# A hybrid trunk layer's expert weights, loaded as four neighbouring rows per partition instead of four rows 128 apart

## What is computed

```python
def expert_choice_ffn(x, w_router, w1, w3, w2):
    cap = EC_FACTOR * T // N_EXPERTS
    aff = jax.nn.softmax(jnp.einsum('btd,de->bte', x, w_router).astype(F32), axis=-1)
    gval, idx = lax.top_k(jnp.swapaxes(aff, 1, 2), cap)
    xs = jax.vmap(lambda xb, ib: xb[ib])(x, idx)
    hid = jax.nn.silu(jnp.einsum('becd,edf->becf', xs, w1)) * jnp.einsum('becd,edf->becf', xs, w3)
    yo = jnp.einsum('becf,efd->becd', hid, w2) * gval[..., None].astype(x.dtype)
    ...
def trunk_layer(x, mod, lp, li, ctx):
    shift1, scale1, gate1, shift2, scale2, gate2 = [mod[:, i, None, :] for i in range(6)]
    h = rmsnorm(x, lp['g_norm1']) * (1 + scale1) + shift1
    mix, new_ctx = token_mixers(h, lp, li, ctx)
    x = x + gate1 * mix
    h2 = rmsnorm(x, lp['g_norm2']) * (1 + scale2) + shift2
    x = x + gate2 * expert_choice_ffn(h2, lp['w_router'], lp['w_e1'], lp['w_e3'], lp['w_e2'])
```

## Time and profile before

| | us |
|---|---|
| median of three runs | 2092.44 |
| lowest and highest run | 2089.23, 2095.91 |
| span of the profiled execution | 2094.6 |
| TensorE busy in it | 1974.3 (94%) |
| expert part of layer 0, first expert product to the end of the last | 572.2 to 1044.4 |
| expert part of layer 1 | 1610.2 to 2081.5 |

### The profile page before, as it was taken

How to read it: one execution, slowest core, us unless ns; L and a number is a source line. 1 busy time by engine, 2 the same in 40 slices (tenths; PEclk the granted TensorE clock), 3 DMA queues, 4 the chain that set the end, 5 groups by cost and what they waited for, 6 DMA issues and landing times. The chain is left out here.

```text
span 2094.6 us, 19778 instructions
## 1 busy us (share of the span) xinstructions
PE 1974.3 (94%) x7810; PEld 896.4 (43%) x7810; DVE 478.2 (23%) x1254; ACT 355.3 (17%) x920; POOL 21.8 (1%) x40
## 2 busy tenths in 40 slices
PE   6999999989899999999979999999898999999997
PEld 2464444454533433433335544544545343334332
DVE  1043224353300100100020612254523011001002
ACT  2123222411200100100021231223112010001000
POOL 0000000000000000000000000000000000000000
PEclk8999999989799999999989999999897999999999
DMA  9141113343799999999952412035346999999996
GB/s 370 61 166 66 60 41 121 152 172 120 264 364 409 396 410 410 409 410 410 409 202 67 165 60 80 21 121 201 123 162 259 377 410 397 410 410 409 410 410 264
DMA packets 136068, 532.95 MB, mean 254 GB/s; under 512 B 5121, under 2 KB 5249, under 8 KB 136001
## 3 DMA queue, kind: packets, MB, share of 16 engines
q1 hardware_dynamic: 134448, 527.59, 64.2%
q0 software_dynamic: 1552, 4.44, 0.6%
HBM read 529.13 MB, written 2.88 MB: 254 GB/s over the span
## 5 line engine op out<-in xcount | busy, mean ns | idle before, releaser
L562 PE MATMUL bank<-ring,hT 128*128 128x512 f32 (+2 forms) x1440 | 598.8, 569 | 3.4 <-DMA ring<-in_w_in 2.1
L562 PE MATMUL bank<-ring,scr 128*64 128x512 f32 (+1 forms) x2176 | 525.9, 597 | 33.8 <-DMA ring<-in_w_e 16.5
L562 PE MATMUL bank<-scr 128*64 128x512 f32 (+6 forms) x2048 | 522.2, 520 | 7.9 <-DVE dsm L1726 4.7
L562 PEld LDWEIGHTS bank<-ring,hT 128*128 128x128 f32 x1440 | 268.7, 191 | 272.2 <-issue 266.1
L562 PEld LDWEIGHTS bank<-scr 128*64 128x64 f32 (+3 forms) x2048 | 213.1, 164 | 295.4 <-issue 287.0
L562 PEld LDWEIGHTS bank<-ring,scr 128*64 128x64 f32 (+1 forms) x2176 | 177.1, 142 | 353.5 <-issue 316.7
L1869 DVE TENSOR_TENSOR scr<-scr,bank 128x512 f32<-128x512 f32 x32 | 22.0, 687 | 627.8 <-ACT scr L1384 627.8
L571 PE MATMUL bank<-cst,scr 128*128 128x128 f32 (+1 forms) x530 | 92.2, 290 | 21.2 <-DVE scr L1764 8.4
L571 PEld LDWEIGHTS bank<-cst,scr 128*128 128x128 f32 (+1 forms) x530 | 58.5, 142 | 101.1 <-issue 70.7
L1384 ACT ACTIVATE scr<-bank 128x512 f32<-128x512 f32 x32 | 19.1, 597 | 467.8 <-PE bank L562 467.8
L562 PE MATMUL bank<-ring,csw 128*32 128x512 f32 x384 | 59.9, 768 | 30.4 <-DMA ring<-in_w_ada 17.7
(11 more groups left out here) (206 smaller groups left out, 1016.6 us busy)
## 6 DMA issues: line engine op xcount, KB each, us to landing
ring<-in_w_e SPq DMA_DIRECT2D x124, 2048.0 KB, 18.2
scr<-in_w_e SPq DMA_DIRECT2D x64, 2048.0 KB, 16.7
ring<-in_w_ada SPq DMA_DIRECT2D x24, 2048.0 KB, 9.7
ring<-in_w_in SPq DMA_DIRECT2D x20, 2048.0 KB, 8.1
ring<-in_w_br SPq DMA_DIRECT2D x8, 1024.0 KB, 7.1
ring<-in_w_out SPq DMA_DIRECT2D x4, 2048.0 KB, 8.8
ring<-in_w_in SPq DMA_DIRECT2D x4, 1552.0 KB, 16.4
ring<-in_w_in SPq DMA_DIRECT2D x4, 1536.0 KB, 6.9
```

What stands on the lines that cost most here:

```text
L562: ins = pe.matmul(out, lhsT, rhs, start=start, stop=stop, **kw)
```

## The change

A half of an expert's matrix is now read with `w.rearrange("(p k) n -> p (k n)", k=4)`: partition p gets rows 4p to 4p + 3, which are 16 KB in one run. The product of chunk k then sums over rows 4p + k, so everything that is multiplied with such a chunk is taken at every fourth element: the helper `quads(ap, k)` gives channels 512h + 4p + b (k = 4h + b). It is applied to the stationary pieces of `xn` in `gather`, to the pieces of `xn` that `widths("h2T")` transposes, and to the row results in `columns(3)` and `columns(4)`; `hid` is written as before and its transposes take every fourth column. The router's weights and the columns of the experts' norm (g_norm2 and two biases) must be in the same order: `wr` is loaded in runs of four rows, and a new tile `cq` gets its 24 columns by 24 small transfers per layer on GpSimd's queue, of 32 partitions x 4 elements, each element 288 B from the next in HBM. VectorE waits for them (`params_second`) ahead of `columns(3)`. No computation is added or left out.

```diff
@@ -155,6 +155,7 @@
         cp = sb("cp", [P, NCOL])
+        cq = sb("cq", [P, 3, KD])
         ca = sb("ca", [P, NCACHE])
@@ -249,7 +250,7 @@
         hs = exp_take(HALF)
-        hid = exp_take(HALF).rearrange("p (b n) -> p b n", b=4)
+        hid = exp_take(HALF).rearrange("p (n b) -> p n b", b=4)
         hidT = exp_take(HALF).rearrange("p (b n) -> p b n", b=4)
@@ -274,6 +275,10 @@
         banks = [ctx.enter_context(nc.psum_tensor(f"bank{i}", [P, 512], F32)) for i in range(8)]
+
+        def quads(ap, k):
+
+            return ap[:, (k // 4) * HALF:(k // 4 + 1) * HALF].rearrange("p (n b) -> p b n", b=4)[:, k % 4, :]
@@ -311,6 +316,7 @@
         params = sem("params")
+        params_q = sem("params_second")
         kv_out = sem("kv_out")
@@ -438,7 +444,11 @@
                         base = li * PER[s]
-                    load(base + before, s, (w_e1, w_e3, w_e2)[s // 2][li, e, (s % 2) * HALF:(s % 2 + 1) * HALF, :], D)
+                    w = (w_e1, w_e3, w_e2)[s // 2][li, e, (s % 2) * HALF:(s % 2 + 1) * HALF, :]
+                    if not (isinstance(base + before, int) and base + before == 0):
+                        sp.wait_ge(freed[s], base + before)
+                    sp.dma_start((ring[:, s] if s < SLOTS else more[:, s - SLOTS]).rearrange("p k n -> p (k n)"),
+                                 w.rearrange("(p k) n -> p (k n)", k=4)).then_inc(loaded[s], 16)
@@ -450,8 +460,8 @@
                     for k in range(4):
-                        r = s * HALF + k * P
-                        sp.dma_start(chunk(SLOTS_E + s, k), w_e1[li, 1, r:r + P, :]).then_inc(loaded[SLOTS_E + s], 16)
+                        rows4 = w_e1[li, 1, s * HALF:(s + 1) * HALF, :].rearrange("(p k) n -> k p n", k=4)
+                        sp.dma_start(chunk(SLOTS_E + s, k), rows4[k]).then_inc(loaded[SLOTS_E + s], 16)
                 for e, slots in ((2, (0, 1)), (1, (2, 3, 4, 5)), (2, (2, 3, 4, 5))):
@@ -500,7 +510,13 @@
                 pool.dma_start(ca[:, :], caches[li, :, :]).then_inc(params, 16)
-                pool.dma_start(wr[:, :, :], w_router[li, :, :].rearrange("(k p) e -> p k e", p=P)).then_inc(params, 16)
+                pool.dma_start(wr.rearrange("p (h b) e -> p h b e", h=2), w_router[li, :, :].rearrange("(h p b) e -> p h b e", h=2, b=4)).then_inc(params, 16)
+                for a in range(4):
+                    for i, c0 in enumerate((COLS["gn2"][0], COLS["bada"][0] + 16, COLS["bada"][0] + 24)):
+                        for h in range(2):
+                            src = colp[li, :, c0 + 4 * h + a].rearrange("(q b) -> q b", b=4)
+                            pool.dma_start(cq[32 * a:32 * a + 32, i, 4 * h:4 * h + 4], src,
+                                           allow_slow_non_contiguous=True).then_inc(params_q, 16)
@@ -619,7 +635,7 @@
                     for k in range(KD):
-                        mm(b[:, 2 * k:2 * k + 2], rsb[:, v % 2, k * P:(k + 1) * P], c_("sel"),
+                        mm(b[:, 2 * k:2 * k + 2], quads(rsb[:, v % 2, :], k) if v > 2 else rsb[:, v % 2, k * P:(k + 1) * P], c_("sel"),
                            signal=big if k == KD - 1 else None)
@@ -647,7 +663,7 @@
                         for t in range(NT):
-                            turn(b[:, t * P:(t + 1) * P], xn[:, t, k * P:(k + 1) * P],
+                            turn(b[:, t * P:(t + 1) * P], quads(xn[:, t, :], k) if name == "h2T" else xn[:, t, k * P:(k + 1) * P],
                                  signal=big if t == NT - 1 else None)
@@ -989,7 +1005,6 @@
                     for k in range(KD):
-                        cols = slice(k * P, (k + 1) * P)
                         b = banks[6 + k % 2]
@@ -999,11 +1014,11 @@
                             pe.wait_ge(sc_ready, 1)
-                        mm(b[:, 0:16 * n], xn[:, 0, cols], Sc[:, e0:e1, :])
+                        mm(b[:, 0:16 * n], quads(xn[:, 0, :], k), Sc[:, e0:e1, :])
                         if k == 0:
                             pe.wait_ge(hot_ready, 1)
-                        mm(b[:, 16 * n:48 * n], xn[:, 1, cols], Sl[:, 0, e0:e1, :], stop=False)
-                        mm(b[:, 16 * n:48 * n], xn[:, 2, cols], Sl[:, 1, e0:e1, :], start=False, signal=gath)
+                        mm(b[:, 16 * n:48 * n], quads(xn[:, 1, :], k), Sl[:, 0, e0:e1, :], stop=False)
+                        mm(b[:, 16 * n:48 * n], quads(xn[:, 2, :], k), Sl[:, 1, e0:e1, :], start=False, signal=gath)
@@ -1052,7 +1067,7 @@
                     for b in range(4):
-                        turn(banks[6][:, b * P:(b + 1) * P], hid[:, b, :], signal=ht_ready if b == 3 else None)
+                        turn(banks[6][:, b * P:(b + 1) * P], hid[:, :, b], signal=ht_ready if b == 3 else None)
                     if not (isinstance(e, int) and e == 0):
@@ -1491,15 +1506,17 @@
                     n = (0, 1, None, 2, 3)[v]
+                    if v == 3:
+                        dve.wait_ge(params_q, (li + 1) * 16 * 24)
                     b = grab(("col", v))
-                    bias = cp[:, COLS["bada"][0] + 8 * n:COLS["bada"][0] + 8 * n + 8]
+                    bias = cp[:, COLS["bada"][0] + 8 * n:COLS["bada"][0] + 8 * n + 8] if v < 2 else cq[:, n - 1, :]
                     gave(("col", v), V.tensor_tensor(modc[:, n, :, :], b[:, 0:16].rearrange("p (k g) -> p k g", g=2),
...
                         V.scalar_tensor_tensor(gs[:, i, :, :], modc[:, 2 * i + 1, :, :], 1.0,
-                                               rep(cp[:, 8 * i:8 * i + 8], 2, 2), ALU.add, ALU.mult).then_inc(mod1, 1)
+                                               rep(cp[:, 0:8] if i == 0 else cq[:, 0, :], 2, 2), ALU.add, ALU.mult).then_inc(mod1, 1)
                         dve.wait_ge(mod1, i + 1)
@@ -1866,7 +1883,7 @@
                     dve.wait_ge(silu_ready, e + 1)
-                    V.tensor_tensor(hid.rearrange("p b n -> p (b n)"), hs, banks[7][:, :], ALU.mult).then_inc(hid_ready, 1)
+                    V.tensor_tensor(hid.rearrange("p n b -> p (n b)"), hs, banks[7][:, :], ALU.mult).then_inc(hid_ready, 1)
                     dve.wait_ge(sg_ready, e + 2)
```

## The result

The changed kernel is slower: 2109.72 us, median of 4 runs (2105.9 to 2112.55), against 2094.18 us for the kernel before (4 runs). The ratio is 1.0071, with a 95% interval of 1.0051 to 1.009, so the change costs 0.7% where 0.7% of gain was forecast. It lies at the upper edge of the stated range, which was rival 1's 2109 us. The profiled execution took 2111.45 us, 2.1 us over its span.

What follows compares the result with a forecast made beforehand. Full DMA engines bound most of the expert part, TensorE waiting for weights; 2094.6 - 19.5 (waits) + 4.7 (transposes) = 2079.8 us profiled, 2077.6 us against the median of runs, range 2071 to 2111.

Steps and rivals of the forecast that it cites:

- rival 1: TensorE's reads at every fourth element are slow in every load, not only in transposes: 2109 us with doubled loads; chance 0.20.
- TensorE's waits as the cap of the gain: Expert parts of both layers: faster transfers can give back only TensorE's waits for weights, 19.5 us.
- 0.13 us per half: Expert loads: each half must land this much sooner, 5.00 for 5.13 us, to remove all 10.1 us of layer 0's waits.
- The rate: Full DMA queue with 16 KB runs: extrapolated from two measured rates to 421 or 425 GB/s, from 409 or 410.
- The 24 small transfers: GpSimd's queue: issuing them takes 13 to 22 us per layer, hidden by other time, so they cost nothing.
- Rivals 2 (cut packets): Transfer engines cut each run into 4 KB packets, so the weights still bound the expert part: 2092 to 2096 us; chance 0.17.
- 4 (slow long packets): Expert loads: 16 KB packets are slow, a half takes 8.7 us, and the kernel over 2600 us; chance 0.10.
- rival 3: Expert loads: a run's fixed part is smaller than two rates say, 1.75% more rate, 2083 us; chance 0.08.
- the one on the stationary operands: TensorE's reads at every fourth element: slow reading would show on transposes first, so +4.7 us there, nothing on gathers and columns.
- the term put at nothing: Gathers and columns(3) and (4) on TensorE: reading at every fourth element was forecast to cost nothing there.
- The last sign of being wrong: TensorE's trace: the forecast is wrong if loads of the stationary pieces of xn are longer than before.
- the middle of two ends: 64 + 24 transposes per layer: cost between 0 and 9.5 us in all, with no row nearer to either, so +4.7 us.

Runs made afterwards that it cites:

- plain gathers: The changed kernel with the stationary pieces of the three gathers read at neighbouring elements again: 2083.67 us, ratio 0.9961 to the kernel before.
- plain columns: The changed kernel with only the row results in columns(3) and (4) read at neighbouring elements again: 2102.28 us, ratio 1.0037 to the kernel before.

## Why the prediction was wrong

**What was right.** TensorE's waits as the cap of the gain: 19.5 us forecast, 19.8 measured, and the long runs alone make the kernel faster by 1.1%. That 0.13 us per half suffices: a half takes 4.88 us at 430 GB/s, 0.25 less than at 409. The rate was estimated as 421 to 425; the extrapolation was a little short. The 24 small transfers cost nothing: 13.01 us (13 to 22 expected), the memset at 55.44 (56 to 65), ScalarE's first write of xbc as before. Rivals 2 (cut packets) and 4 (slow long packets) are out by 0.62 us per packet of 16 KB, rival 3 by the waits, which went whole. Two counts were off, and nothing hung on them: 188 of the 192 halves go in long runs, not 184, and five packets reach 8 KB in the earlier trace rows, not four. By the Trainium skill, "DMA: Bandwidth & Descriptors", section "Why small descriptors are slow (HBM only)", a packet costs some three cycles beside its data; the estimate from that figure was 1.75%. The traces show 5% (409 to 430 GB/s), so a run of 4 KB pays for more than these three cycles.

**The step that failed** is the one on the stationary operands: "The records of the gathers take each column in two steps, the transposes in one, so the slow reading would show on transposes first; the gathers also leave TensorE time between banks", and from it "I put nothing on gathers and columns". It is the other way round: the term put at nothing, the gathers and columns with what follows them, is nine tenths of the price. The transposes' loads did become longer (140 to 212 ns in h2T), but a load lies beside the product before it, and the spacing grew by 0.005 us in h2T and by 0.02 us per transpose in hid. The gathers' loads, already busy for 8.79 of TensorE's 9.33 us, became 1.7 times as long and are now all of it: 48 x 0.229 us is 11.0, where 11.50 were measured. The row that would have told stood in the text: six loads of 0.115 us in 1.03 us leave 0.34, and doubled loads need 1.38. I wrote this spare time down as a cover and didn't ask whether it covers a doubling. The last sign of being wrong that I had named, longer loads of the pieces of xn, is what the trace shows. Columns(4), where 0.115 us a load was the whole pace, came out at 0.229, exactly twice.

**Rival 1 was the case, and its total came out by luck, since its errors cancel.** It had 18 us per layer; measured are 16.7 and, in layer 1, 16.5. Its terms, with what layer 0 shows in brackets: columns(4) 1.8 (1.8), two full-clock gathers 5.5 (6.5), the first gather 6 (2.2), the transposes 4.7 (1.6). For the first gather it took the middle between doubled loads at full clock and at half clock. The low end was the case, which is 1.7 us by its own figures (48 x 0.23 less 9.33) and not 1: at a granted clock of 0.70 a slow load took hardly longer than at 1.00. What the rival did not have is the clock: behind slow loads the granted clock falls to the lower level, and work that reads neighbours pays, 2.5 + 0.3 us behind columns(4) and 3.3 in two experts behind gathers, less 1.6 in the router's products. The kernels with plain gathers and with plain columns show this as cause and effect, each for its own stretch. Which of the three gathers is followed by a slow expert changes from kernel to kernel, and that stays open; so do the few us at the start of each layer.

By the Trainium skill, "SBUF — State Buffer", section "Door 1: The DMA port swizzle (why `[64,N]` ≈ `[32,N]`)", lines of 16 bytes want two hits or more. The table above agrees for the loads of the gathers: two hits are nearly free (196 ns for 190), one hit is 329. The loads of the transposes don't fit it: with two hits they are at 209 ns for 140 already. The same section says that float32 can be strided for free up to four; here that holds up to two. I gave rival 1, this page's case, 0.20 because no row showed it. Whether it decides the sign hung on one number that no row had, the price of a slow load, and for the transposes I took the middle of two ends, which is no measurement either.

## What to carry to other kernels

Before a layout change makes TensorE's stationary operand strided, compare the load's pace with the pace of the product in each group: where they are near (few moving columns: gathers, two-column products) a doubled load shows (columns(4) 2.0 times as long, a gather 1.4 times), where the product covers it little is left (0.02 us or less per transpose). In the columns float32 at every second element cost 5% here, at every third 1.5 and at every fourth 2.0 times. If a transfer wants another order, let an engine with idle time write it scattered (here +349 ns per 128 x 512 on VectorE, hidden), and leave TensorE its neighbours. And a gain at one bound is capped by the waits there, but a new cost at the other engine is not: it is paid wherever that engine already leads.

## What the runs showed of the hardware that I had not expected

- Slow stationary loads lower TensorE's granted clock: 16 of them ahead, and the next 24 transposes run at 0.50 where they had 1.00 (2.82 to 5.36 us).
- A float32 load of 128 columns costs by the 16-byte pieces touched: columns(4) paces a record at 0.115, 0.121, 0.176, 0.229 and 0.233 us at every 1st, 2nd, 3rd, 4th and 8th element.
- Loads of transposes become longer at every second element already (140 to 209 ns), where those of the gathers hardly do (190 to 196), and at every eighth they aren't longer still (192). Why is open.
- With loads at every fourth element a gather's time hardly depends on the clock: 11.7 us at a mean granted clock of 0.70, 11.5 at 1.00.
- Runs of 16 KB in place of 4 KB in each partition lift a full queue from 409 to 430 GB/s.
